# Modulation row sums as plain fp32 on four column groups, and the last gate moved to the feed-forward stage

## The reference

```python
sc_lat, sc_ctx = silu(c), silu(c_ctx)
m_l = sc_lat @ w_ada + b_ada              # w_ada is 1024 x 6144
m_c = sc_ctx @ w_ada + b_ada
sh1, sc1, g1, sh2, sc2, g2 = split(m_l, 6); csh1, csc1, ... = split(m_c, 6)
hl = rmsnorm(lat, norm_g[0]) * (1 + sc1) + sh1
hc = rmsnorm(cx, norm_g[0]) * (1 + csc1) + csh1
q, zf_fwd, zf_bwd, v, g = split(h @ w_in, 5)   # for both; 8 heads, chunked scan
lat = lat + g1 * hgrn2(hc, hl)
lat = lat + g2 * conv_ffn(modulate(rmsnorm(lat, norm_g[1]), sh2, sc2))   # d_ff 2816
x = second_block(rmsnorm(lat, final_g))        # retention + window attention, MLP 4096
```

## Time and profile before

| | us |
|---|---|
| median of 3 runs (lowest, highest) | 919.49 (916.34, 919.61) |
| profiled execution | 918.26 |
| its span, first to last instruction | 916.4 |
| PE / DVE / ACT busy in it | 901.9 / 656.2 / 492.8 |

### The profile page before, as it was taken

One profiled execution on the slowest core, in us unless ns is written; L12 is line 12 of the kernel. 1 busy time (PEld: TensorE's weight loads), 2 busy tenths in 40 slices (PEclk: granted clock), 3 DMA queues, 4 the chain that ended last, 5 costly groups with the idle time before them and its releaser, 6 DMA issues.

```text
span 916.4 us, 17024 instructions
## 1 busy us (share of the span) xinstructions
PE 901.9 (98%) x6286; PEld 820.7 (90%) x6286; DVE 656.2 (72%) x1101; ACT 492.8 (54%) x769; POOL 0.2 (0%) x4
## 2 busy tenths in 40 slices
PE   8999999999999999999999999999999999999997
PEld 4478888888899999999999998999999889999996
DVE  4977688888886876676677988876576766555555
ACT  4632566666664755555556545445464664444443
POOL 0000000000000000000000000000000000000000
PEclk9999999999999999999999999999999999999999
DMA  9858644443425265655655543345446356555551
GB/s 338 314 188 315 258 139 138 139 137 137 137 92 185 83 215 172 199 177 170 200 178 166 182 143 126 129 162 176 159 150 215 129 186 205 185 187 189 187 185 51
DMA packets 45582, 160.86 MB, mean 176 GB/s; under 512 B 5216, under 2 KB 6624, under 8 KB 45408
## 3 DMA queue, kind: packets, MB, share of 16 engines
q1 hardware_dynamic: 43488, 156.27, 50.3%
q10 hardware_dynamic: 2048, 3.97, 1.2%
HBM read 159.16 MB, written 1.05 MB: 175 GB/s over the span
## 4 chain that ended last, share of the span: by engine, by line
PE 86%; DVE 4%; DMA 4%; ACT 3%; issue 2%; SPq 0%; DVEq 0%; ACTq 0%
PE bank L439 21%; PE bank L441 20%; PE bank L440 20%; PE bank L505 4%; PE bank L507 4%; PE bank L506 4%; DMA raw<-in_stream 2%; DMA arena<-in_ada 2%; DVE arena L1592 1%; PE bank L1265 1%; ACT w_hi L426 1%; PE bank L1307 1%; PE bank L1287 1%; PE bank L1303 1%; PE bank L1267 1%
## 5 line engine op out<-in xcount | busy, mean ns | idle before, releaser
L433 DVE TENSOR_TENSOR w_lo<-raw,w_hi 128x1024 fp32r<-128x1024 f32 x252 | 304.3, 1222 | 133.8 <-ACT w_hi L426 133.3
L439 PE MATMUL bank<-h_hi,w_hi 128*128 128x256 f32 (+1 forms) x1232 | 369.5, 300 | 2.8 <-DVE w_lo L433 1.9
L441 PE MATMUL bank<-h_hi,w_lo 128*128 128x256 f32 (+1 forms) x1232 | 363.1, 295 | 0.0
L440 PE MATMUL bank<-h_lo,w_hi 128*128 128x256 f32 (+1 forms) x1232 | 361.6, 293 | 0.0
L426 ACT ACTIVATE w_hi<-raw 128x1024 fp32r<-128x1024 f32 x252 | 261.1, 1051 | 133.6 <-PE bank L441 86.9
L439 PEld LDWEIGHTS bank<-h_hi,w_hi 128*128 128x128 f32 x1232 | 232.3, 189 | 13.1 <-issue 2.9
L440 PEld LDWEIGHTS bank<-h_lo,w_hi 128*128 128x128 f32 x1232 | 234.1, 190 | 6.4
L441 PEld LDWEIGHTS bank<-h_hi,w_lo 128*128 128x128 f32 x1232 | 231.6, 188 | 5.8
L439 PE MATMUL bank<-y_hi,w_hi 128*128 128x256 f32 x304 | 86.6, 285 | 0.0
L441 PE MATMUL bank<-y_hi,w_lo 128*128 128x256 f32 x304 | 86.0, 283 | 0.0
L440 PE MATMUL bank<-y_lo,w_hi 128*128 128x256 f32 x304 | 85.4, 281 | 0.0
(11 more groups left out here) (259 smaller groups left out, 1118.4 us busy)
## 6 DMA issues: line engine op xcount, KB each, us to landing
raw<-in_stream SPq DMA_DIRECT2D x252, 512.0 KB, 3.4
arena<-in_ada SPq DMA_DIRECT2D x32, 512.0 KB, 5.2
xres<-in_ada SPq DMA_DIRECT2D x8, 512.0 KB, 3.3
tok<-in_tok SPq DMA_DIRECT2D x3, 512.0 KB, 8.5
con<-in_con ACTq DMA_DIRECT2D x1, 1472.0 KB, 9.8
xres<-in_tok ACTq DMA_DIRECT2D x1, 1024.0 KB, 8.5
out<-arena SPq DMA_DIRECT2D x4, 256.0 KB, 2.1
...
```

What stands on the lines that cost most here:

```text
L433: dve.tensor_tensor(w_lo[c.slot][:, :], raw[c.slot][:, :], w_hi[c.slot][:, :].bitcast(F32), ALU.subtract).then_inc(S("split_lo"), 1)
L439: pe.matmul(dst, hi_w, a_hi, start=start, stop=False, skip_group_check=True)
L440: pe.matmul(dst, hi_w, a_lo, start=False, stop=False, skip_group_check=True)
L441: return pe.matmul(dst, lo_w, a_hi, start=False, stop=stop, skip_group_check=True)
```

## The change

All four quarters are now plain fp32. The two silu columns of each k stand in a zeroed stationary operand of COL = 32 columns, and the matmul of k writes rows 32 (k % 4) to 32 (k % 4) + 31 of the bank: each quarter is 8 matmuls of 32 x 512 on four groups of rows, whose four partial sums DVE adds after the transposes (which are 128 x 128 now). The stream loses its eight modulation chunks (N_HEAD = KT), so their splits on ACT and DVE go; the sixteen quarter tiles come through eight buffers, in turn with the value chunks. The sums of quarter q + 1 stand inside value tile q, as do its transposes. For quarters 1 to 3 ACT writes the modulated tokens in fp32 (`modulate_wide`) and then copies them to fp32r; DVE only subtracts. GROUPS is 1: one sixth is summed during the values; the last gate's eight tiles are loaded and summed in the peeled part of the feed-forward stage and turned into columns between its last two down tiles. The matmuls that run ahead of the first data (`warm`) are six of 512 columns and six of 128 instead of eight of 128, and the fillers between quarter 0's tiles are 6, 8, 3 and 4 instead of 6, 3 and 3.

```diff
-GROUPS = 2
+QUARTERS = 4
+GROUPS = 1
-N_HEAD = 2 * KT
+N_HEAD = KT
-WARM = 8
-FILL = (6, 3, 3)
-PLAIN = 2
+WARM = 6
+FILL = (6, 8, 3, 4)
+COL = 32
+GATE_ROWS = (0, 1, 1, 2, 2, 2)
...
             def load_ada(i):
                 row = (ADA - ADA_FIRST + i) * P
-                sp.dma_start(ada_raw[i], ada_in[row:row + P, :]).then_inc(S(f"ada_in{i}"), 16)
+                if i >= KT:
+                    sp.wait_ge(S("ada_summed"), i // 4 - 1)
+                sp.dma_start(ada_raw[i % KT], ada_in[row:row + P, :]).then_inc(S(f"ada_in{i % KT}"), 16)
...
+            for q in range(1, QUARTERS):
+                for i in range(4 * q, 4 * q + 4):
+                    load_ada(i)
+                load_one(q)
...
+            def load_gate(k):
+                if k >= 4:
+                    sp.wait_ge(S("gate_summed"), k - 3)
+                sp.dma_start(gate_raw[k % 4], ...)
+            with sp.Fori(i_head + HEADS, i_ffn + 1) as i:
+                load_stream(i)
+            sp.wait_ge(S("y_full"), HEADS)
+            for k in range(4):
+                load_gate(k)
+            for u in range(1, 4):
+                load_stream(i_ffn + u)
+                for k in (2 * u, 2 * u + 1) if u >= 2 else ():
+                    load_gate(k)
...
+            def modulate_wide(q):
+                act.wait_ge(S("mod_first"), q + 1)
+                for k in (2 * q, 2 * q + 1):
+                    act.wait_ge(S("tok_normed"), k + 1)
+                    for at, gain, shift in ((k * TC, gain_l, mod), (k * TC + T, gain_c, mod_c)):
+                        act.activation(wide[:, at:at + T], tok[:, at:at + T], ACT.Identity, scale=gain[:, k:k + 1],
+                                       bias=shift[:, k:k + 1]).then_inc(S("tok_wide"), 1)
+                for k in (2 * q, 2 * q + 1):
+                    x = slice(k * TC, (k + 1) * TC)
+                    act.wait_ge(S("tok_wide"), 2 * (k - 2) + 2)
+                    act.activation(h_hi[:, x], wide[:, x], ACT.Copy).then_inc(S("h_hi"), 2)
...
-            def ada_plain(first, end):
+            def ada(first, end):
                 for i in range(first, end):
                     q = i // 4
-                    pe.wait_ge(S(f"ada_in{i}"), 16)
+                    pe.wait_ge(S(f"ada_in{i % KT}"), 16 * (i // KT + 1))
                     for b in range(2):
                         k = 2 * (i % 4) + b
-                        last = pe.matmul(psum[4 + q][0:2, :], cs_pairs[:, k, :], ada_raw[i][:, b * 512:b * 512 + 512],
-                                         start=k == 0, stop=k == KT - 1, skip_group_check=True)
+                        at = COL * (k % 4)
+                        last = pe.matmul(psum[4 + q][at:at + COL, :], cs_cols[:, k, :], ada_raw[i % KT][:, b * 512:b * 512 + 512],
+                                         start=k < 4, stop=k >= 4, skip_group_check=True)
...
-            values(0, {(0, 3): lambda: ada_plain(5, KT), (1, 2): lambda: turn_rows(1)})
-            ada_rows(2)
-            values(1, {(0, 2): lambda: turn_rows(2)})
-            ada_rows(3)
-            values(2, {(0, 2): lambda: turn_rows(3)})
+            ada(4, 6)
+            warm(FILL[3])
+            values(0, {(0, 3): lambda: ada(6, 8), (1, 2): lambda: turn_rows(1)})
+            values(1, {(0, 3): lambda: ada(8, 12), (1, 2): lambda: turn_rows(2)})
+            values(2, {(0, 3): lambda: ada(12, 16), (1, 2): lambda: turn_rows(3)})
...
+                if t == JF - 2:
+                    pe.wait_ge(S("gate_summed"), KT)
+                    mod_columns(gate_sum, psum[6], T).then_inc(S("gate_columns"), 1)
```

More of the change, by code:

```diff
@@ L270, in build @@
         gain_2 = tiny(KT)
+        part_sum = [tiny(2 * 4) for _ in range(QUARTERS)]
         eps_sq = tiny(1)
@@ L311, in build @@
         mod_sum = [part(D) for _ in range(GROUPS)]
-        mod_raw = [part(D) for _ in range(2 * GROUPS)]
-        mod_rows = [xres[:, q * 512:(q + 1) * 512] for q in range(4)]
-        ada_raw = [mod_raw[-1]] + [part(D) for _ in range(KT - 1)]
-        zeros = part(P)
+        mod_raw = [part(D) for _ in range(4)]
+        mod_rows = [xres[:, q * 512:(q + 1) * 512] for q in range(QUARTERS)]
+        ada_raw = [part(D) for _ in range(KT)]
+        cs_w = part(COL * KT)
+        zeros = mod_sum[0][:, 0:512]
         used[0] = TC
@@ L320, in build @@
         m_relu = [part(T) for _ in range(2)]
+        used[0] = 4096
+        gate_sum = part(D)
+        gate_raw = [part(D) for _ in range(4)]
         used[0] = TC
@@ L405, in build @@
         v_all = tok
[L406 to L408 removed]
+        cs_cols = cs_w[:, :].rearrange("p (k w) -> p k w", w=COL)
         cs_pairs = cs.rearrange("p (k w) -> p k w", w=2)
@@ L1172, in token_sum @@
                 pe.matmul(psum[1][:, :], ones, wide[:, 0:TC], start=True, stop=True).then_inc(S("tok_summed"), 1)
-            def ada_rows(q):
-                for i in range(4 * q, 4 * q + 4):
-                    c = Chunk(split_number(i))
-                    pe.wait_ge(S("split_lo"), c.n + 1)
-                    for b in range(2):
-                        k = 2 * (i % 4) + b
-                        for part_ in (w_hi, w_lo):
-                            last = pe.matmul(psum[4 + q][0:4, :], cs_w[:, 4 * k:4 * k + 4], part_[c.slot][:, b * 512:b * 512 + 512],
-                                             start=k == 0 and part_ is w_hi, stop=k == KT - 1 and part_ is w_lo,
-                                             skip_group_check=True)
-                    last.then_inc(S("multiplied"), 1)
             def turn_rows(q):
                 pe.wait_ge(S("mod_rows"), q + 1)
-                n = row_parts(q)
                 for m in range(4):
-                    last = pe.transpose(psum[TURN_BANKS[q]][:, n * m:n * m + n], mod_rows[q][0:n, m * P:m * P + P],
-                                        ident[0:n, 0:n])
+                    last = pe.transpose(psum[TURN_BANKS[q]][:, m * P:m * P + P], mod_rows[q][:, m * P:m * P + P], ident)
                 last.then_inc(S("mod_turned"), 1)
             def values(j, between={}):
-                c, half = Chunk(value_number(j)), j // 4
+                c, half = Chunk(j), j // 4
                 pe.wait_ge(S("split_lo"), c.n + 1)
@@ L1676, in _ @@
                 low_tokens(k)
-            norm_tokens(2)
-            norm_tokens(3)
-            for n in range(1, 4):
-                lo(dve, Chunk(n))
+            lo(dve, Chunk(1))
+            for k in range(2, KT):
+                norm_tokens(k)
+            lo(dve, Chunk(2))
+            quarter(1)
             dve.tensor_tensor(lb_m, p1("lb0", 0, 16), p1("lb1", 0, 16), ALU.max).then_inc(S("lb_step"), 1)
@@ L1945, in _ @@
                     lo(dve, Chunk(c, 2 + AHEAD))
+                for k in range(sum(GATE_ROWS[:j]), sum(GATE_ROWS[:j + 1])):
+                    gate_tile(k)
             with dve.Fori(0, (JF - FFN_PEEL) // 4) as i:
@@ L2229 @@
     w = a["w_ada"][0].reshape(KT, P, 6, D)
-    ada = np.concatenate([w[:, :, g:g + 2].transpose(0, 2, 1, 3).reshape(2 * KT, P, D) for g in (2, 4)])
+    ada = np.concatenate([w[:, :, 2], w[:, :, 3:5].transpose(0, 2, 1, 3).reshape(2 * KT, P, D), w[:, :, 5]])
     hg = _columns(a["hg_w_in"][0]).reshape(5, HEADS, P, D)
@@ L2253 @@
     first = np.concatenate([_quarter(x, 0) for x in first])
-    ada = np.concatenate([ada, first[:KT]])
-    stream = np.concatenate([v[:1], first[KT:KT + 4], v[1:2], first[KT + 4:], v[2:], heads, _rows(a["hg_w_out"][0]), np.stack(ffn),
+    ada = np.concatenate([ada, first])
+    stream = np.concatenate([v, heads, _rows(a["hg_w_out"][0]), np.stack(ffn),
                              in2, _rows(a["w_swa_out_2"][0]), _rows(a["w_ret_out_2"][0]), _rows(a["w_out_2"][0]), np.stack(mlp)])
```

217 lines of the change are left out of this document (97 added, 120 removed).

## The result

| | before | after |
|---|---|---|
| median (lowest, highest), 5 runs each | 918.60 (916.34, 919.61) | 924.83 (923.80, 925.22) |
| ratio after / before, 95% interval | | 1.0071 (1.0058 to 1.0083) |
| span of the profiled execution | 916.4 | 922.7 |
| start of the values stage | 21.33 | 21.41 |
| end of the values stage, head 0 starts | 82.09 | 90.76 |

A forecast was written before the change was run, and what follows sets the result against it. PE, busy 98% of the span, was taken to bound the kernel. Terms +5.35 (values), -4.5, +1.9 (column sums), +2.0 and +2.5 gave +7.2: 918.3 + 7.2 = 925.5 us, range 914 to 933 (8 in 10).

The forecast's parts named there:

- Row sums: Values stage on PE: 13.0 us removed, 4.8 added, as matmuls on four row groups run beside each other; -8.2.
- the prediction's rival: Row-sum matmuls: each record runs beside one neighbour only, 3.9 us per 8 matmuls, total 929.5 us; chance 0.13.
- Transposes: Values stage: four 128 x 128 blocks a quarter take 0.9 instead of 0.3; +1.7, and +0.45 for the start.
- Gaps: PE waits before value tiles 1, 2 and 3: 5.5 and 0.2, then 3.0 each; +11.4 net, bounds 3 and 15.
- Clock: Values stage: granted clock falls to 1.2 GHz after PE's waits; +2.5 us, bounds 0 and 5.
- Head 0: From values end to head 1: 19.6 us instead of 24.1, with 8 DVE tiles and one group; -4.5.
- Feed-forward stage: First iterations: eight modulation tiles make DVE up to 6 us late, 4 us slack; PE stops +2.0, bounds 0 and 6.
- The signs: Profile after: 1.9 us sums, waits ended by h_hi, values end 87 to 89, w_lo waits around 350 to 370 us.
- the second sign: Profile after: head 1 starts within 3 us of 106.16.
- The cheap gaps: Before value tiles: ACT and DVE have tokens ready before PE asks; 910 to 917 us, chance 0.17.
- Half overlap: Row sums: 8 matmuls take 9 records of 0.44, 3.9 us; total 929.5 us, chance 0.13.
- no overlap: Row sums: fp32 matmuls on different groups run serially, 7.0 us a quarter; total 941 us, chance 0.05.

The follow-up runs named there:

- The kernel with filled gaps: Changed kernel plus 28, 10 and 10 unused 128-column matmuls in front of value tiles 1, 2 and 3; 921.09 us, ratio 1.0031.
- The kernel with the gate's move alone: Kernel before with only GROUPS = 1 and the last gate's loads, sums and column sums in the feed-forward stage, quarters untouched; 915.55 us, ratio 0.9970.
- the kernel with the spread gate: Changed kernel with the gate's eight tiles one each in iterations 1 to 8 of the feed-forward stage; 922.29 us, ratio 1.0036.
- the kernel with its gaps closed: Changed kernel with h_hi straight from tokens, quarter 1 ahead of norms 4 to 7 and chunk 2, quarter 2's sums and the transposes earlier; 906.50 us, ratio 0.9873.

## Why the prediction was right, and where it was not

**The mechanism held.** PE's removed work came back as gaps, because the split quarters had been the cover under which ACT and DVE made the next tokens. Closing the gaps by order and by the direct `h_hi`, with the sums and the gate as the change has them, turns +6 us into -12.

**Row sums, predicted -8.2.** Measured 0.99 + 1.86 + 1.86 = 4.7 from start to start (24.39 to 25.38, 41.29 to 43.15, and the same for quarter 3) against the old 12.9: -8.2. The bet on full overlap from line 1276's two records was right, and one, two and four groups settle it. The page TensorE: Matmul & The Clock Gate of the Trainium skill (Part 3, "The mechanism") has matmuls start and end strictly in program order. If that held for each record, with the two of an fp32 matmul on one group, two groups and four would both take 3.9 us; the runs show 3.63 and 1.92, so it doesn't hold for the records. For whole matmuls it can still hold: two or four of 0.88 us side by side would make 3.5 and 1.8 us, so the prediction's rival went further than the Trainium skill does. The runs have 1.9 and 3.7 times for two and four groups; the 2.38 times for three that the Trainium skill states (the same page, "Measured speedup vs the span model") lies between them, and no run here has three.

**Transposes, predicted +1.7, and +0.45 for the start of the values: mis-sized by 2.1.** The four 128 x 128 transposes of a quarter are one row of x4, and the next matmul starts 0.35 us later (27.60 to 27.95). The step read the row of line 1257 in the earlier trace rows as two transposes of two records each; it is four transposes of one record. They cost what the small ones cost (0.33 and 0.34), and the values start at 21.41, not 21.8.

**Gaps, predicted +11.4; measured +12.4.** That is 12.7 and twice 0.15 for `h_lo`, less what before had at value tile 1, 0.33 and a wait of 0.25 for `h_lo` that the prediction left out. Gaps 2 and 3 were worked out as 2.8 and 0.2 for `h_lo`; they are 2.76 and 0.15 (49.73 to 50.12 instead of 0.24). Gap 1 was given 5.5 and is 7.16: PE was free 1.1 us earlier (28.9, not 30.0, partly the transposes' error), and chunk 2 landed at 30.4, not 29.6. Work that PE no longer does ahead of a wait that another engine ends is not gained, it only makes the wait longer: part of the transposes' error came back in gap 1. The landing does set the gap here, as the step had it: DVE idles 1.64 ahead of chunk 2's `w_lo`. What the step didn't see is that DVE's six norms stand right behind it and hold the gap at 5.42 when chunk 2 is early.

**Clock, predicted +2.5; measured 3.75.** The term was mis-sized, within its bounds of 0 and 5. The lower level stands from 34.2 to 41.0 us and from 61.5 to 64.9 us. Twelve matmuls take 5.23 behind gap 1 instead of the 2.98 of value tile 0 (21.41 to 24.39), 2.25 more, and 4.67 instead of some 3.2 behind gap 3, 1.5 more. The kernel with filled gaps gives 3.7 for it by the time.

In all the values stage ends 8.67 later against 5.35 + 2.5 = 7.85. The measured terms give -8.2 + 0.1 + 12.4 + 3.75 = 8.05. Most of the 0.6 that is left is in the brackets, which end at the modelled end of a matmul: from start to start, less 0.235 for the matmul itself, the three gaps are 7.3 + 2.9 + 2.9 = 13.1 and not 12.7.

**Head 0, predicted -4.5.** 110.17 - 90.76 = 19.41 against 24.07: -4.66. The kernel with the gate's move alone has 19.40 (81.91 to 101.31), and the granted clock stays at 1.00 there. The column sums that came back were taken at 1.9 and are 1.71.

**Feed-forward stage, predicted +2.0; measured +2.02.** The three brackets say 1.06 in all, but from start to start the stage is 2.02 longer without the column sums, and the kernel with the spread gate has 1.96 of it back. The stops come where the iterations have two tiles. The term was right, with bounds of 0 and 6 around it.

**The sum.** 8.67 - 4.66 = 4.0 at head 1. From there to the feed-forward stage the changed kernel takes 0.2 less (110.17 to 314.16 against 106.16 to 310.37), in the stage 2.02 + 1.71 more, and behind it the 1.22 of the kernel before are gone, which no step had: 6.3, which is what the span is longer by. What follows takes 414.17 us in both. The errors partly cancelled, and that was luck: transposes and start 2.1 too much and the 1.22 not seen, gaps 1.0 and clock 1.25 too little. The total was nearer than its terms.

**The signs.** The sums in 1.9 us, the gaps and what ends them, and the stops for `w_lo` (364 to 374 us) came as listed. Two did not: the values end at 90.76 and not at 87 to 89, and head 1 starts 4.0 later and not within 3 us. The terms themselves had 5.35 + 2.5 - 4.5 = 3.35 at head 1, so the second sign did not fit them even then; the rest is the gaps and the clock.

**The rivals.** The cheap gaps (911 to 914 us) failed by 9 us: it needed all gaps under 3.6, and they are 12.7. Its sum was sound, though: the kernel with its gaps closed comes to 906.5, where the rival's 911.3 held 2.1 of transposes and start that are not there, and lacked the 1.22 gained behind the feed-forward stage. Half overlap (3.9 us for a quarter) and no overlap would have given 929.5 and 941. Four groups in 1.92 us rule both out. The kernels with two groups and one come to 929.5 and 938; the first agreement is a coincidence, since its quarters take 3.63 and its lower clock and opening differ too.
